# Layer opening of a two-layer mixer step: filter tiles waited for one by one in a new order, the adaLN bias on GpSimd, the first filter network in halves, no copy of x

## The chip, the cores and the metric

The kernel runs on one core of a Trainium2 chip. The metric is the device time of one execution in microseconds; of before there are three runs. The engines are TensorE (PE), VectorE (DVE), ScalarE (ACT), GpSimd (POOL) and SyncE (SP, which here issues nearly all DMAs).

## What is computed

Two layers (DEPTH = 2) of a diffusion backbone over 1024 sample tokens and 128 prompt tokens, 1024 channels, float32. Each layer is one mixer with four groups (latent attention, grouped-query attention, differential attention, a Hyena long convolution). What matters here is the beginning of a layer:

```python
def hyena_filters(n, lp):
    feats = concatenate([t, cos(f * w), -sin(f * w)])                  # n x 33
    h = sin(freq[0] * (feats @ fw1 + fb1))                             # n x 64
    h = sin(freq[1] * (h @ fw2 + fb2))                                 # n x 64
    h = (h @ fw3).reshape(n, 2, 2, 256)                                # two orders, forward and backward
    return h * exp(-t * abs(decay))

mod = silu(c) @ ada_w[i] + ada_b[i]                                    # shift, scale, gate; once for c, once for c_ctx
h = rmsnorm(x, norm_pre) * (1.0 + scale) + shift
out = mixer(h, ...)                                                    # its Hyena part convolves with the filters by FFT
x = x + gate * rmsnorm(out, norm_post)
```

The output is x after both layers, and some keys and values of the prompt.

## The kernel before

Tokens lie in nine tiles of 128: tile t < 8 holds the sample tokens with residue t modulo 8, tile 8 (NT) the prompt. One SBUF area, the arena, holds nearly everything at fixed offsets. PSUM has eight banks, which TensorE claims in turn (`K.claim`, `K.next`): a claim waits until the bank's last user has been drained. Each engine has its own program, in a fixed order; semaphores join them.

The opening of a layer has these steps.

*Network.* Two small products (`network_product`, K = 33 and 64), each followed on VectorE by scaling and a range reduction (`network_angle`: tensor_scalar, tensor_scalar, three scalar_tensor_tensor, tensor_scalar, each waited for) and on ScalarE by a sine (L1302). The 1152 tokens lie as 2 x 576 columns; the arithmetic runs over all 576 at once, though the products come in 512 and 64. For layer 1 the network runs inside the output stage of layer 0, beside the output products of tiles 4 and 6.

*Decays.* ScalarE makes exp(-t |decay|) of each tile: Abs (L1307), nine Exp (L1309). In layer 0 after the sines, in layer 1 after the last square of layer 0.

*Filter transforms.* For order o = 1 and then 0, TensorE multiplies the nine tiles with fw3, tiles 0 to 8 in sequence, jobs `("f3", o, t)`. VectorE (`filter_rows`) multiplies each bank with the decay (L1722) and, for even t, folds forward and backward part into difference and sum (two more L1722); tiles 0 and 8 have a small memset (L1828) in between. For odd t ScalarE negates the backward part (L1321).

*Filter spectra.* For each order 8 banks `("FE", o, a0, p)`, a0 = 0 to 3 and p = 0, 1, and a prompt bank `("FEp", o)`. a0 even reads tiles a0 and a0 + 4; a0 odd reads all four odd tiles, with the negated parts. TensorE starts them once all tiles are ready:

```python
pe.wait_ge(*S.at("filter_negated", o))
pe.wait_ge(*S.at("filter_folded", (o, NT)))
```

ScalarE drains the banks scaled (L1335, L1340). After order 1, VectorE and GpSimd add and subtract the quarters (`butterfly`) into a spectrum that is stored away; ScalarE drains order 0 only after that.

*Modulation.* ada(j), j = 0 to 5, multiplies silu(c) with 512 columns of ada_w; its left operand is csil, spread at L1764 and L1765 over 256 columns of the arena in each layer. ada(0) follows the transforms of order 1, ada(1) to (3) lie between its spectrum banks, ada(4) and (5) in order 0. VectorE adds the bias (`add_ada_bias`) over 128 partitions, of which GpSimd had cleared all (L2381) and SyncE filled two; SyncE waits for the clearing with ada_b and what is queued behind. Small products bring shift and scale onto partitions (job modT), and, before the last FE pair of order 0, the gates onto rows (`gate_row`), which VectorE multiplies with norm_post (`gate_rows`) and SyncE stores away (gates_kept).

*x.* Six of nine rows tiles are loaded (`load_x`), squared on ScalarE (L1315), scaled on VectorE (`normalize`, with a power on GpSimd), turned by TensorE (`x_turned`) and modulated by ScalarE (L1347) and VectorE (`modulate`, L1806) into hT. The first product of the Hyena input, `hyena_input(0, 0)`, needs tiles 0 to 3. In layer 0 x is first copied by DMA into the output xs[0], and read from there. SyncE loads x rows 6 to 8 after the store of the gate rows.

## Time and profile before

| what | us |
|---|---|
| median of three runs | 2441.25 (2438.95 to 2441.79) |
| profiled execution | 2435.95 |
| its span | 2434.2 |
| TensorE busy | 2272.0 (93%) |
| VectorE, ScalarE, GpSimd busy | 1317.5, 935.4, 253.8 |

Layer 0 opens with the span; its first product of the Hyena input starts at 123.09. Layer 1 opens at 1220.6. In a row of the timeline, the first number is the start from the beginning of the span, the second the time to the end of what is merged in the row; in brackets stands how long the engine was idle before it, and what ended that. L1722, L2336 and L659 are helpers (tensor_tensor of VectorE and of GpSimd, matmul): the tiles and shapes tell one use from another. A float32 matmul stands as two records of MATMUL.

### The profile page before, as it was taken

How to read it: one execution, taken by the hardware profiler on the slowest of the kernel's cores; microseconds unless marked ns; L12 is line 12 of the kernel's file. 1: busy time of each engine (PE TensorE's matmuls, PEld its weight loads, DVE VectorE, ACT ScalarE, POOL GpSimd, SP SyncE). 2: the span in 40 equal slices, each digit the busy share in tenths (PEclk: the TensorE clock that was granted, in tenths of full speed). 3: DMA queues.
4: the chain of work that ended last, by engine and by line, in shares of the span. 5: the costliest groups of instructions: out<-in, count | busy, mean ns of one | idle time of the engine just before them, and what ended most of it. 6: DMA issues, size and time to landing. Idle time of an engine off the chain costs nothing. (4 is left out here: it accounts for less than half of the span.)

```text
span 2434.2 us, 36385 instructions
## 1 busy us (share of the span) xinstructions
PE 2272.0 (93%) x14536; PEld 1599.2 (66%) x14536; DVE 1317.5 (54%) x2454; ACT 935.4 (38%) x1924; POOL 253.8 (10%) x400
## 2 busy tenths in 40 slices
PE   6999999899999998989999999998999999889898
PEld 3656865685477776864856577657854777768657
DVE  3642764564656466583446337545645654855732
ACT  2332113553155265483224221135521652744721
POOL 0310001000100011011304000010011000110213
PEclk9999999999999999999989999999999999999999
DMA  8710100100020000113275101001001100001022
GB/s 282 262 46 29 57 18 1 54 2 15 2 76 2 4 4 7 36 36 131 79 233 203 53 11 57 18 1 54 1 15 37 41 1 8 1 7 71 1 87 87
DMA packets 75150, 129.64 MB, mean 53 GB/s; under 512 B 25794, under 2 KB 38978, under 8 KB 73348
## 3 DMA queue, kind: packets, MB, share of 16 engines
q1 hardware_dynamic: 73960, 121.65, 14.6%
q10 hardware_dynamic: 1024, 5.67, 0.7%
q8 instruction: 117, 1.92, 0.3%
q14 instruction: 49, 0.40, 0.1%
HBM read 110.10 MB, written 21.92 MB: 54 GB/s over the span
## 5 line engine op out<-in xcount | busy, mean ns | idle before, releaser
L659 PE MATMUL psum<-arena 128*32 128x128 f32 (+9 forms) x9392 | 1505.3, 391 | 63.0 <-issue 11.9
L659 PEld LDWEIGHTS psum<-arena 128*32 128x32 f32 (+3 forms) x9392 | 930.5, 151 | 564.5 <-issue 423.7
L663 PE MATMUL psum<-ident,arena 128*128 128x128 f32 (+1 forms) x2248 | 335.2, 279 | 70.8 <-ACT arena L1543 34.0
L1722 DVE TENSOR_TENSOR arena<-arena 128x256 f32<-128x256 f32 (+10 forms) x710 | 318.8, 493 | 146.6 <-ACT arena L1419 42.6
L663 PEld LDWEIGHTS psum<-ident,arena 128*128 128x128 f32 (+1 forms) x2248 | 254.3, 141 | 155.6 <-issue 101.9
L659 PE MATMUL psum<-k_parts,q_parts 96*128 96x384 f32 (+2 forms) x1000 | 269.8, 366 | 17.1 <-ACT arena L1454 6.0
L2019 DVE TENSOR_REDUCE st<-psum 128x1 f32<-128x1152 f32 (+1 forms) x144 | 177.9, 1237 | 52.3 <-PE psum L659 52.1
L1722 DVE TENSOR_TENSOR arena<-psum,arena 128x512 f32<-128x512 f32 (+2 forms) x116 | 68.1, 596 | 253.3 <-PE psum L659 253.1
L2114 DVE TENSOR_REDUCE st<-psum 128x1 f32<-128x1152 f32 (+1 forms) x144 | 174.0, 1235 | 53.6 <-PE psum L659 53.1
L659 PEld LDWEIGHTS psum<-k_parts,q_parts 96*128 96x128 f32 (+1 forms) x1000 | 171.0, 193 | 34.7 <-issue 16.8
L1454 ACT ACTIVATE arena<-psum,st 128x1152 f32<-128x1152 f32 (+1 forms) x144 | 162.4, 1128 | 51.8 <-DVE st L2019 43.7
L1529 ACT ACTIVATE arena<-psum,st 128x1152 f32<-128x1152 f32 (+1 forms) x144 | 162.5, 1129 | 34.0 <-DVE st L2114 33.6
L1469 ACT COPY arena<-psum 128x512 f32<-128x512 f32 (+1 forms) x244 | 102.1, 433 | 184.9 <-PE psum L663 184.8
L2336 POOL TENSOR_TENSOR st<-st,minus 128x1 f32<-128x1 f32 x72 | 43.7, 607 | 798.2 <-ACT arena L1529 798.2
L2336 POOL TENSOR_TENSOR arena<-arena 128x1024 f32<-128x1024 f32 (+2 forms) x38 | 98.6, 2603 | 189.1 <-DVE arena L1855 138.7
L2033 DVE COPY arena<-psum 128x512 f32<-128x512 f32 (+1 forms) x156 | 93.6, 612 | 28.7 <-PE psum L663 28.7
L1543 ACT COPY arena<-psum 128x512 f32<-128x512 f32 (+1 forms) x200 | 90.3, 470 | 46.4 <-PE psum L663 45.4
L1886 DVE SCALAR_TENSOR_TENSOR arena<-arena,hcw 128x1024 f32<-128x1024 f32 x24 | 30.8, 1285 | 125.9 <-ACT arena L1373 125.5
L2124 DVE SCALAR_TENSOR_TENSOR arena<-arena,st 128x1152 f32<-128x1152 f32 (+1 forms) x72 | 93.0, 1291 | 9.8 <-POOL st L2336 9.8
L1492 ACT ACTIVATE arena<-psum 128x512 f32<-128x512 f32 x36 | 21.5, 598 | 173.3 <-PE psum L659 173.3
L2336 POOL TENSOR_TENSOR st<-st,mhalf 128x1 f32<-128x1 f32 (+2 forms) x72 | 56.2, 780 | 300.8 <-DVE st L1727 300.8
L1653 ACT CAST q_parts<-psum 96x512 fp32r<-96x512 f32 (+1 forms) x54 | 31.7, 588 | 117.0 <-PE psum L663 116.5
(146 smaller groups left out, 1685.8 us busy)
## 6 DMA issues: line engine op xcount, KB each, us to landing
arena<-in_ada_w SPq DMA_DIRECT2D x12, 2048.0 KB, 8.3
arena<-in_w_in SPq DMA_DIRECT2D x10, 2048.0 KB, 9.6
arena<-out_xs SPq DMA_DIRECT2D x36, 512.0 KB, 5.9
out_xs<-arena SPq DMA_DIRECT2D x18, 512.0 KB, 2.6
arena<-in_w_out SPq DMA_DIRECT2D x4, 2048.0 KB, 8.0
out_xs<-in_x ACTq DMA_DIRECT2D x1, 4608.0 KB, 19.2
spectrum_kept<-arena SPq DMA_DIRECT2D x2, 2304.0 KB, 8.6
arena<-spectrum_kept SPq DMA_DIRECT2D x2, 2304.0 KB, 8.4
```

What stands on the lines that cost most here:

```text
L659: return nc.tensor.matmul(out, lhsT, rhs, start=start, stop=stop)
L663: return nc.tensor.transpose(out, src, ident[0:n, 0:n])
L1454: nc.scalar.activation(at(buf, nk, w), psum[:, 512 * b0:512 * (b0 + nk)].rearrange("p (c n) -> p c n", c=nk)[:, :, 0:w], ACT.Exp, bias=st[ ...
L1469: nc.scalar.copy(at(SLOTS[grp] + slot(grp, u) * 1152 + 512 * j, nk * P), bank[b][:, 0:nk * P]).then_inc(*S.up("turned_scalar", (grp, number)))
L1529: nc.scalar.activation(at(buf, nk, w), psum[:, 512 * b0:512 * (b0 + nk)].rearrange("p (c n) -> p c n", c=nk)[:, :, 0:w], ACT.Exp, bias=st[ ...
L1543: nc.scalar.copy(at(SLOTS[grp] + slot(grp, u) * 1152 + 512 * j, nk * P), bank[b][:, 0:nk * P]).then_inc(*S.up("turned_scalar", (grp, number)))
L1722: return nc.vector.tensor_tensor(out, a, b, op)
L2019: nc.vector.tensor_reduce(st[:, 16 + x % 4:17 + x % 4], psum[:, 512 * b0:512 * (b0 + nk)].rearrange("p (c n) -> p c n", c=nk)[:, :, 0:w], ...
L2033: nc.vector.tensor_copy(at(SLOTS[grp] + slot(grp, u) * 1152 + 512 * j, nk * P), bank[b][:, 0:nk * P]).then_inc(*S.up("turned_vector", (grp ...
L2114: nc.vector.tensor_reduce(st[:, 16 + x % 4:17 + x % 4], psum[:, 512 * b0:512 * (b0 + nk)].rearrange("p (c n) -> p c n", c=nk)[:, :, 0:w], ...
L2124: nc.vector.scalar_tensor_tensor(p0, p1, c, p0, ALU.mult, ALU.add).then_inc(*S.up("mixed", (grp, u)))
L2336: return nc.gpsimd.tensor_tensor(out, a, b, op)
```

## The change

- The nine tiles are taken in the order 2, 6, 0, 4, 8, 1, 5, 3, 7 (FILTER_ORDER), the spectrum products in the order 2, 0, 1, 3 (FE_ORDER). An even a0 waits only for tile a0 + 4 folded, an odd one for tile 7 and the negations. The prompt's product stands after the second a0, which in order 1 ScalarE's negations of tiles 3 and 7 follow too.
- ScalarE drains ada(j), GpSimd adds the bias over two partitions. The clearing memset and its wait are gone; ada_b is loaded after the last output product of the layer before.
- The gate rows are made after all spectrum banks of order 0, and on VectorE after `normalize` of six tiles.
- The silu columns of layer 1 are made in the output stage of layer 0, at another place in the arena. A table load for Exp is asked for after the second sine there.
- The first network runs in two halves of 288 columns. The decay row and negt are loaded first on ScalarE's queue, and in layer 0 the decays are made ahead of the sines; tanh for silu follows the sines, and VectorE finishes silu at the prompt tile of order 1.
- x isn't copied: layer 0 reads the input itself, and xs has two instead of three entries. `load_x` waits for tile 7 of order 0 instead of tile 8.

```diff
+FILTER_ORDER = (2, 6, 0, 4, NT, 1, 5, 3, 7)
+FE_ORDER = (2, 0, 1, 3)
-HALF_PARTS = ((0, 512), (512, HALF - 512))
+HALF_PARTS = ((0, HALF // 2), (HALF // 2, HALF // 2))
...
 # SyncE
-                sp.wait_ge(*S.at("ada_bias_cleared"))
+                if l >= 1:
+                    sp.wait_ge(*K.full(("y", NT, 1), 1))
                 for s in range(2):
-                    load(at(A_ADAB, 3072, parts=1, base=s), lay("ada_b"), "ada_params")
+                    load(at(A_ADAB, 3072, parts=1, base=s), lay("ada_b"), "ada_bias")
...
-                if l == 0:
-                    sp.wait_ge(S.raw("x_copied"), 16)
-                else:
+                if l >= 1:
...
-                sp.wait_ge(*K.emptied(("f3", 0, NT)))
+                sp.wait_ge(*K.emptied(("f3", 0, FILTER_ORDER[-1])))
...
 # TensorE
-                    for t in range(TT):
+                    for t in FILTER_ORDER:
...
-                    pe.wait_ge(*S.at("filter_negated", o))
-                    pe.wait_ge(*S.at("filter_folded", (o, NT)))
-                    for a0 in range(4):
+                    for turn, a0 in enumerate(FE_ORDER):
                         back = (4 - a0) % 4
-                        if o and a0 % 2:
-                            ada((a0 + 1) // 2)
-                        if o == 0 and a0 == 2:
+                        if a0 % 2:
+                            pe.wait_ge(*K.emptied(("f3", o, 7)))
+                            pe.wait_ge(*S.at("filter_negated", o))
+                        else:
+                            pe.wait_ge(*S.at("filter_folded", (o, a0 + 4)))
+                        if o and turn % 2:
+                            ada((turn + 1) // 2)
+                        if o == 0 and turn == 2:
                             ada(5)
...
+                        if turn == 1:
+                            pe.wait_ge(*S.at("filter_folded", (o, NT)))
+                            ps = claim(("FEp", o), K.next())
...
+                    else:
+                        pe.wait_ge(*S.at("ada_biased", 5))
+                        for s in range(2):
+                            for half in range(2):
+                                ps = claim(("gate_row", s, half), K.next())
...
 # ScalarE
+            load_decay(act, 0, "decay_params")
+            act.dma_start(negt[:, :], I["negt"]).then_inc(*S.up("decay_params", None, 16))
             load_rest(act, 0, "first_rest")
+            act.wait_ge(*S.all("decay_params"))
+            decays()
+            for n in (1, 2):
+                for i, (c, w) in enumerate(HALF_PARTS):
+                    act.wait_ge(*S.at("first_angle", (n, i)))
+                    nc.scalar.activation(at(F_ARG + c, w), at(F_ARG + c, w), ACT.Sin).then_inc(*S.up("first_sine", (n, i)))
             act.wait_ge(S.raw("constants"), 16 * N_CONST)
             nc.scalar.activation(csil[:, :, :], craw[:, :, :], ACT.Tanh, scale=0.5).then_inc(S.raw("silu_ready"), 1)
-            act.dma_start(xs[0], I["x"]).then_inc(S.raw("x_copied"), 16)
...
+                def take_ada(j):
+
+                    act.wait_ge(*K.full(("ada", j)))
+                    nc.scalar.copy(mod[:, j * 512:(j + 1) * 512], B(("ada", j))).then_inc(*K.drained(("ada", j)))
...
+                    take_ada(0 if o else 4)
                     if o == 0:
+                        negate((1, 5, 3, 7))
...
+                        if o and turn == 0:
+                            negate((1, 5))
+                        if turn == 1:
+                            if o:
+                                negate((3, 7))
+                            act.wait_ge(*K.full(("FEp", o)))
+                            nc.scalar.mul(at(B2 + 4096, 512), B(("FEp", o)), 1.0 / N_PROMPT).then_inc(*K.drained(("FEp", o)))
+                    if o:
+                        take_ada(3)
...
+                            if n == 2:
+                                nc.scalar.preload_act_table_set("natural_log_exp_and_others")
...
 # VectorE
                 filter_rows(1)
-                add_ada_bias(0)
-                add_ada_bias(1)
-                add_ada_bias(2)
-                add_ada_bias(3)
                 filter_rows(0)
-                add_ada_bias(4)
                 for o in (1, 0):
                     if o == 0:
                         modulation()
-                        add_ada_bias(5)
-                        gate_rows()
                         for t in range(RING):
                             normalize(t)
+                        gate_rows()
...
 # GpSimd
-                nc.gpsimd.memset(at(A_ADAB, 3072), 0.0).then_inc(*S.up("ada_bias_cleared"))
+                def bias_ada(j):
+
+                    pool.wait_ge(*S.at("ada_bias"))
+                    pool.wait_ge(*K.emptied(("ada", j)))
+                    m = at(A_MOD + j * 512, 512, parts=2)
+                    tt(m, m, at(A_ADAB + j * 512, 512, parts=2), ALU.add).then_inc(*S.up("ada_biased", j))
+
                 for o in (1, 0):
+                    for j in range(4) if o else (4,):
+                        bias_ada(j)
```

## Rows read from the trace of the kernel before

**Rows 1.** The page: busy us, share of the span, instructions.
```profile
PE 2272.0 (93%) x14536; PEld 1599.2 (66%) x14536; DVE 1317.5 (54%) x2454; ACT 935.4 (38%) x1924; POOL 253.8 (10%) x400
```
**Rows 2.** Windows: busy PE, PEld, DVE, ACT, POOL; clock, DMA share, GB/s.
```profile
0.00:23.60 23.60, 4.37 (x16) 1.52 (x16) 10.14 (x19) 4.14 (x6) 2.99 (x7) 1.00 0.88 282
23.60:43.40 19.80, 19.74 (x37) 5.90 (x37) 11.11 (x22) 6.86 (x16) 0.00 (x0) 1.00 0.98 315
43.40:82.00 38.60, 38.60 (x190) 24.07 (x186) 11.52 (x22) 6.79 (x13) 0.00 (x0) 1.00 0.68 220
...
1220.60:1229.00 8.40, 7.48 (x19) 2.65 (x18) 6.81 (x7) 5.97 (x13) 5.50 (x3) 1.00 1.03 377
1229.00:1239.40 10.40, 5.64 (x19) 1.12 (x19) 9.84 (x21) 1.67 (x4) 0.00 (x0) 0.50 0.76 230
```
**Rows 3.** Timeline of layer 0's opening: start, us, engine, instruction, idle before.
```profile
7.40 2.19 PE L659 MATMUL psum<-arena 33*64 33x512 f32 x8 [7.40 <-DMA fwp<-in_hy_freq]
...
14.80 0.68 ACT L1302 ACTIVATE arena<-arena 128x576 f32<-128x576 f32 x1 [1.44 <-DVE arena L1738]
...
23.66 17.22 PE L659 MATMUL psum<-arena 64*128 64x512 f32 x24 [5.94 <-ACT arena L1302]
...
45.99 0.60 ACT L1335 ACTIVATE arena<-psum 128x512 f32<-128x512 f32 x1 [6.65 <-PE psum L659]
```
**Rows 4.** Groups by form, 0 to 45 us: busy us, mean ns, idle before.
```profile
L1737 DVE SCALAR_TENSOR_TENSOR arena<-arena 128x576 f32<-128x576 f32 x6 | 4.5, 758 | 0.2
...
L1309 ACT ACTIVATE arena<-arena,negt 128x256 f32<-128x256 f32 x9 | 3.7, 494 | 0.0
...
L1746 DVE TENSOR_SCALAR arena<-psum,fwp 128x512 f32<-128x512 f32 x2 | 1.6, 810 | 12.8 <-PE psum L659 12.8
...
L1296 ACT ACT_TABLE_LOAD x1 | 1.3, 1283 | 6.2 <-issue 6.2
...
L1735 DVE TENSOR_SCALAR arena<-arena 128x576 f32<-128x576 f32 x2 | 0.9, 460 | 0.1
...
L1307 ACT ACTIVATE arena<-arena 128x256 f32<-128x256 f32 x1 | 0.4, 398 | 0.0
```
**Rows 5.** Timeline of layer 1's opening, 1220 to 1245 us.
```profile
1220.61 7.47 PE L659 MATMUL psum<-arena 64*128 64x512 f32 x18
...
1223.99 2.35 POOL L2336 TENSOR_TENSOR arena<-arena 128x1024 f32<-128x1024 f32 x1 [1.58 <-DVE arena L2084]
1224.16 4.81 DVE L1765 COPY arena<-csil 128x16 f32<-128x16 f32 x1
...
1226.29 2.66 POOL L2381 MEMSET arena<- 128x3072 f32 x1
...
1229.41 0.88 DVE L1722 TENSOR_TENSOR arena<-arena 128x256 f32<-128x256 f32 x2
...
1231.05 3.64 PE L659 MATMUL psum<-arena 128*32 128x512 f32 x16
...
1238.26 0.88 DVE L1722 TENSOR_TENSOR arena<-arena 128x256 f32<-128x256 f32 x2
...
1239.40 12.97 PE L659 MATMUL psum<-arena 128*128 128x256 f32 x58 [4.71 <-DVE arena L1722]
...
1244.74 0.60 ACT L1335 ACTIVATE arena<-psum 128x512 f32<-128x512 f32 x1 [1.05 <-PE psum L659]
```
**Rows 6.** Timeline of layer 0: a negation, modT, the end of the opening.
```profile
75.48 0.42 ACT L1321 ACTIVATE arena<-arena 128x256 f32<-128x256 f32 x1 [4.93 <-DVE arena L1722]
...
97.69 0.16 DVE L1780 COPY mcol<-psum 128x16 f32<-128x16 f32 x1
...
117.65 5.51 DVE L1806 TENSOR_SCALAR arena<-psum,mcol 128x128 f32<-128x128 f32 x17
...
123.09 8.80 PE L659 MATMUL psum<-arena 128*128 128x512 f32 x16 [3.36 <-DVE arena L1806]
```
**Rows 7.** The page's DMA issues: KB each, us from issue to landing.
```profile
gates_kept<-arena SPq DMA_DIRECT2D x2, 1024.0 KB, 14.0
```

More of the change, by code:

```diff
@@ L156 @@
 SPLIT_W = {"gqa": 896, "diff0": 768, "diff1": 768}
-N_CONST = 6
+N_CONST = 5
 BARRIERS = 5
@@ L695, in ada @@
                     weights("ada", j)
-                    if j == 0:
+                    if j == 0 and l == 0:
                         pe.wait_ge(*S.at("silu_columns"))
+                    elif j == 0:
+                        pe.wait_ge(*S.at("silu_columns", "next", 1))
                     ps = claim(("ada", j), K.next())
@@ L721, in _ @@
                     else:
-                        for j in range(4):
-                            pe.wait_ge(*K.emptied(("ada", j)))
+                        if l == 0:
+                            pe.wait_ge(S.raw("constants"), 16 * N_CONST)
+                        pe.wait_ge(*S.at("ada_biased", 3))
                         ps = claim(("modT",), K.next())
@@ L1330, in _ @@
                             act.wait_ge(*S.all(f"x_stored{i}", 1))
-                    for a0 in range(4):
+                    for turn, a0 in enumerate(FE_ORDER):
+                        if o and turn % 2:
+                            take_ada((turn + 1) // 2)
+                        if o == 0 and turn == 2:
+                            take_ada(5)
                         for p in range(2):
@@ L1749, in _ @@
[L1749 to L1765 removed]
+                    network_angle(n, "first_step", "first_angle", (n, i), c, w)
@@ new lines, in silu_columns, with silu @@
+            def silu_columns(key):
+                link(nc.vector.memset(at(A_CSIL, KD * 32), 0.0))
+                nc.vector.tensor_copy(at(A_CSIL, KD, 32)[:, :, 0:2], csil[:, :, :]).then_inc(*S.up("silu_columns", key))
+            def silu():
+                v.wait_ge(S.raw("silu_ready"), 1)
+                nc.vector.scalar_tensor_tensor(csil[:, :, :], csil[:, :, :], 1.0, craw[:, :, :], ALU.add, ALU.mult
+                                               ).then_inc(S.raw("silu_ready"), 1)
+                v.wait_ge(S.raw("silu_ready"), 2)
+                nc.vector.tensor_scalar(csil[:, :, :], csil[:, :, :], 0.5, None, ALU.mult).then_inc(S.raw("silu_ready"), 1)
+                v.wait_ge(S.raw("silu_ready"), 3)
+                silu_columns(None)
@@ L2324, in _ @@
                                 v.wait_ge(*K.emptied(job))
-                            network_angle(n, "vector_step", "angle")
+                            network_angle(n, "vector_step", "angle", n)
+                    if t == NETWORK_AT[1] and l + 1 < DEPTH:
+                        silu_columns("next")
         @block.gpsimd
```

112 lines of the change are left out of this document (47 added, 65 removed).

## The prediction

> **What bounds the kernel now.** Read the page's busy rows first: TensorE is busy 93% of the span [rows 1], so only TensorE's idle or slowed stretches can give time back. The view by windows then compares them [rows 2]. The first 23.6 us hold 4.37 us of TensorE work. In the opening of layer 1, TensorE works 5.64 us of the 10.4 us to 1239.40, and the granted clock is at 0.50 (the 1.2 GHz level) in all of them. In the stretch from 23.60 TensorE is never short of work, but its records are long: the same 18 records of the transforms that take 7.47 us in layer 1 [rows 5] make up most of the 24 that take 17.22 us from 23.66 [rows 3]. So it runs at the lower level too, although the clock column says 1.00 there.
>
> The timelines say who ends the idle stretches. At the start: products, VectorE's angle arithmetic, a sine, the second products, again VectorE and a sine, and only then the filter transforms [rows 3]. In layer 1 the transforms end at about 1228.9 and the last filter tile is folded at 1239.14 (1238.26 + 0.88), 0.26 us before TensorE resumes [rows 5]. VectorE folds one even and one odd tile per 2.1 us (8.85 us for four pairs and one memset), but it has finished its first tile only when GpSimd's memset ends at 1228.95: its tiny copy of csil, begun at 1224.16, lasts 4.81 us beneath GpSimd's add and memset. The 4.71 us wait at 1239.40 is for tiles that the first spectrum product doesn't read.
>
> **Part 1: the filter spectrum in layer 1.** The memset, the copy and VectorE's clearing leave this place (the latter two run at tile 4 of the output stage, beside TensorE's output products; without that cover they would cost up to the 4.81 us of the copy). The tile order is 2, 6, 0, 4, prompt, 1, 5, 3, 7. VectorE is free at about 1223.9 (the copy's start, less its 0.3 us of clearing) and starts tile 2. A product takes 0.6 us (a pair's 2.1 us hold two of them and 0.88 us of folds); the folds read two SBUF tensors and wait for GpSimd's add of x, 1223.99 to 1226.34 [rows 5]. They end at 1227.2, tile 6 at 1228.7, tile 0 at 1230.5 (it has the memset), tile 4 at 1232.0, the prompt tile at 1233.8 and the four odd tiles, 0.6 each, at 1236.2.
>
> TensorE: by 7.47/18 a record of 512 columns takes 0.42 us and one of 256 half of it; a matmul has two, so an even spectrum bank (four matmuls of 256) takes 1.7 us and the prompt's, two, 0.86 with its start. Eight tiles to 1228.08, the ninth 0.83 more (2 x 7.47/18), say 1228.9; ada(0) takes half of 3.64 us if the clock holds, 1230.8. Tile 6 was folded at 1228.7, so product (1, 2) starts at 1230.8. The next ask tile 4 after 3.4 us, at 1234.2 (ready 1232.0), then the prompt's, then tile 7: all ready. The start moves from 1239.40 to 1230.8: 8.6 us. Before, the first two banks ended at 1244.74 (when ScalarE takes the second) where 3.44 us at the full clock would give 1242.9: 1.8 us for the low clock, also saved if the clock doesn't fall.
>
> Against this stands a new wait. In spectrum 1 the negation of tiles 3 and 7 sits on ScalarE behind the drain of the fourth bank: 0.1 + 0.5 + 0.42 + 0.42 = 1.45 us [rows 5, 6], while TensorE has only the prompt product, 0.86 us, before it asks for them. Queued behind that wait are product 1 and everything after it: 0.6 us per layer. Bounds 0 and 1.0; I take 0.6. Layer 1 gives 8.6 + 1.8 - 0.6 = 9.8 us. Bounds: if the clock falls in the transforms anyway (it fell at 1229.0 after an idle of 0.97 us, which now goes; the second transforms of layer 0, between 43.4 and 82 us, ran through at 1.00 [rows 2]), ada(0) costs 1.8 us more and the 1.8 isn't saved, 6.2 us; if contention costs VectorE nothing, nothing is added, since TensorE is the bound.
>
> The Trainium skill, SBUF — State Buffer, "SBUF: two separate sides", calls the port pair that VectorE and GpSimd share an exclusive lock: an instruction of VectorE with two SBUF inputs and a GpSimd one that reads SBUF shut each other out for their whole length. The trace agrees in the copy that waits out both GpSimd instructions [rows 5]. It speaks against biases on GpSimd: each 2 x 512 add could stop VectorE's folds. By that rule the add for ada(0), an estimated 1.3 us by the 2.35 us for 1024 columns halved, moves tile 4 to 1233.3, still ahead of 1234.2: the sum stays. By bounds without it: 0 to 1.3 us of VectorE, 0 of TensorE.
>
> **Part 2: the network in halves, layer 0.** Per half of 288 columns: the read from PSUM 0.58 us (0.81 at 512, less 224 columns at 1.04 ns), three tensor_scalar at 0.31 (0.46 at 576, less 288 columns at half of STT's 1.04 ns), three scalar_tensor_tensor at 0.46 (0.76 less 288 x 1.04 ns), 0.15 between them: 2.95 us [rows 4]. Product half 0 ends at about 8.6 (half of 2.19 after 7.40) and VectorE does 8.6 to 14.5 for n = 1. ScalarE is the catch: it issued nine loads before its first table load at 6.2 [rows 4] and now ten, to 6.8; then come that load (1.28), Abs (0.40) and nine Exp (3.7), to 12.3, and the sine's table, 13.6. The first half sine ends at 14.05, its product at 15.2, VectorE works to 21.1, the last sine ends at 21.65 and the transforms start at 21.7 instead of 23.66: 2.0 us. If Abs and Exp need two tables it is 0.7; if ScalarE weren't late, 2.7. I take 2.0: in the trace Abs ran with no load ahead of it [rows 4]. Loads still land in time: only the first parameters at 7.40 hold TensorE, and two more small transfers ahead on ScalarE's queue could move that by 0 to 0.3 us. I take 0.
>
> All this is ahead of work at the low clock. The clock rose not in the transforms but some 1.7 us after the spectrum products began at 43.4: their first bank came at 45.99, 2.6 us instead of 1.72 [rows 3], so 1.7 us of it ran at half speed; if it rises with the products again, the 2.0 us come through whole; if up to 1.7 us later, 0.8 less. The new wait costs 0.6 here too. Layer 0: 2.0 - 0.6 = 1.4 us, 0 to 2.5.
>
> **Part 3: edits that I cost at nothing.** ada(j) drained by ScalarE (0.6 us each, idle there) and biased by GpSimd: modT asks for it some 10 us after ada(3). VectorE loses its adds of some 0.6 us, none of them waited for. The modT bank is asked for again by the second bank of product 1, about 99.9 by the old clock; VectorE reads modT at 97.7 [rows 6], less the bias add gone ahead of it: 2 us to spare. The four gate rows (3.4 us of TensorE) move behind the spectrum products, and on VectorE behind six normalisations. ScalarE's last square comes 2.6 us earlier, but VectorE then has four products of 0.6 us to do before the bias and modulate(0), which began at 117.65 and sets TensorE's start at 123.09 [rows 6]. 2.6 against 2.5: 0 (-0.6 to 1.0 per layer). The copy of x held nobody: TensorE never waited for a load after 7.40. Its going is worth 0; between 0 and the 0.6 us of its issue.
>
> **Sum.** 9.8 + 1.4 = 11.2 us. The profiled execution took 2435.95 (span 2434.2); it becomes 2424.8. The three runs of before have their median 5.3 us above it, so the forecast is 2441.25 - 11.2 = 2430.0.
>
> **Rivals.** (A) The clock falls in layer 1 all the same, and rises late in layer 0: 6.2 + 0.6 = 6.8 us, 2434.5. For it: it fell once in just these 8.4 us of 64-row matmuls. Against: there was an idle moment right before, and layer 0 shows none. (B) The order doesn't do what it says: some other wait (a bank, a lock) makes TensorE wait for all nine tiles. Then the start is at 1236.2 and at the low clock: 3.2 - 0.6 + 1.4 = 4.0 us, 2437.2. Against it: the banks asked for are drained before the times above. (C) The gate rows make it slower. SyncE stands behind their drain, at about 116.5 now, with the store of them and behind it x rows 6 to 8. If the store holds the loads back for its whole time to land, 14.0 us [rows 7], and row 6, of half its size, takes half as long, row 6 is there at 137.5; a square and the scaling make some 3 us, so x_turned(6) starts at 140.5 where TensorE wants it at 131.9, the end of the product begun at 123.09 [rows 6]: 8.6 us per layer, 17.2 in both, less the gain 6.0 us slower: 2447. It decides from row 6 landing 12.4 us after the store's issue, and eats the gain from 18. Against it: one queue's transfers overlap, and ahead of the store stand weights that will have landed by then.
> (D) More than I count: the gate rows give 1.0 per layer, 0.6 of stall is 0: 2426.8.
>
> **How the numbers follow.** Forecast 2430.0: 0.55. A 0.20, B 0.08, C 0.04, D 0.13. The range: A and D inside, plus 1 us for the spread of the runs (2438.95 to 2441.79): 2425.0 to 2436.5. Outside lie B, C and the tails. This measurement can tell about 0.2%, 4.9 us, from no change. The forecast, D and nearly all of A clear that; B stands just below it and C is beyond. Faster 0.87, same 0.10, slower 0.03.
>
> **What would show it.** Right: the transforms start near 21.7, ScalarE's nine Exp come before its sines; in layer 1 no memset on GpSimd, product (1, 2) 8 to 9 us earlier after the last stage's end, clock at 1.00 throughout; a stall of 0.6 us in front of product 1 ended by ScalarE's negation; modulate(0) as long after the transforms as before. Wrong: a clock of 0.50 after ada(0), TensorE waiting for a fold or the first half sine ended by a second table load, or a wait for x row 6.

## The result and the profile after

The kernel after takes 2409.38 us (median of 4 runs, 2406.51 to 2414.31) where the kernel before takes 2440.1 in the same comparison (2436.34 to 2441.79): ratio 0.9877, 95% interval 0.9858 to 0.9895, some 30 us faster. Forecast were 2430.0 and a range down to 2425.0; the direction was right, the size was not.

The profiled execution after is the slowest of its four (2414.31; span 2412.5), that of before (2435.95; span 2434.2) is below all four of its own, so the two traces show 21.7 us. The repeat below, profiled in one of its fastest runs (span 2404.9), is read beside them. The page's busy rows: TensorE is busy 15.8 us less with the same 14536 instructions [rows 1].

```profile
PE 2256.2 (94%) x14536; PEld 1595.1 (66%) x14536; DVE 1307.9 (54%) x2454; ACT 942.1 (39%) x1939; POOL 264.2 (11%) x410
```

Equal instructions with less busy time mean that single records became shorter or lay over each other. The timeline of TensorE in the two openings of the kernel after (start, us, engine, instruction, idle time before it and who ended it):

```profile
5.89 2.19 PE L666 MATMUL psum<-arena 33*64 33x288 f32 x8 [5.89 <-DMA fwp<-in_hy_freq]
14.19 2.18 PE L666 MATMUL psum<-arena 64*64 64x288 f32 x8 [6.11 <-ACT arena L1322]
22.14 22.36 PE L666 MATMUL psum<-arena 64*128 64x512 f32 x88 [5.77 <-ACT arena L1322]
44.98 25.50 PE L666 MATMUL psum<-arena 128*128 128x256 f32 x132 [0.48 <-issue]
...
1215.12 5.76 PE L666 MATMUL psum<-arena 64*128 64x512 f32 x20
1222.34 11.94 PE L666 MATMUL psum<-arena 128*32 128x512 f32 x68 [1.46 <-DVE arena L1767]
1234.76 25.50 PE L666 MATMUL psum<-arena 128*128 128x256 f32 x132 [0.48 <-issue]
...
1301.28 1.69 PE L666 MATMUL psum<-arena 128*128 128x512 f32 x2 [2.44 <-DVE arena L1852]
```

To be seen: the transforms of layer 1 are 20 records in 5.76 us. Before, 18 took 7.47, and two more followed behind a wait [rows 5]. The wait of 4.71 us for the last folds is gone; in its place stand 1.46 us for a bank that VectorE drains late and, in front of the first odd product, 0.48 us. The weight loads of the same stretch mark where each piece starts:

```profile
1215.11 0.30 PEld L666 LDWEIGHTS psum<-arena 64*128 64x128 f32 x4 [0.35 <-issue]
1215.65 0.19 PEld L666 LDWEIGHTS psum<-arena 64*128 64x128 f32 x1 [0.23 <-issue]
...
1218.03 0.30 PEld L666 LDWEIGHTS psum<-arena 64*128 64x128 f32 x4 [0.81 <-issue]
1218.57 0.19 PEld L666 LDWEIGHTS psum<-arena 64*128 64x128 f32 x2 [0.24 <-issue]
...
1222.30 0.19 PEld L666 LDWEIGHTS psum<-arena 128*32 128x32 f32 x8 [2.26 <-issue]
...
1224.19 3.32 PEld L666 LDWEIGHTS psum<-arena 128*128 128x128 f32 x16 [0.84 <-issue]
```

Four loads lie in 0.30 us, where before two did and the others followed one by one, 0.43 us apart:

```profile
1220.61 0.29 PEld L659 LDWEIGHTS psum<-arena 64*128 64x128 f32 x2 [0.35 <-issue]
1221.14 0.19 PEld L659 LDWEIGHTS psum<-arena 64*128 64x128 f32 x1 [0.24 <-issue]
```

The first spectrum product (the last row of the kernel after) starts 9.08 us after the first transform; before it was 18.79 (1239.40 less 1220.61). No window of this stretch is at the low clock any more:

```profile
1215.10:1224.20 9.10, 7.64 (x38) 2.44 (x37) 7.28 (x13) 4.69 (x12) 2.90 (x2) 1.00 1.03 381
1224.20:1234.40 10.20, 10.08 (x56) 7.08 (x52) 6.34 (x13) 4.63 (x10) 2.56 (x2) 1.00 1.06 371
```

From such rows comes this account. The opening of layer 0 runs from 0, that of layer 1 from its first transform, both to the first Hyena product:

```
us                                   before    after    repeat
layer 0: first transform              23.66    22.14    22.14
  nine transforms                     16.14    10.41    10.09
  ada(0)                               3.57     1.86     1.86
  second nine transforms               8.26     5.69     5.69
  first Hyena product at              123.09   113.14   110.88
layer 1: transform to first product   18.79     9.08     9.07
  second nine transforms               8.26     5.69     5.69
  length of the opening                99.50    86.16    86.16
both openings                          222.6    199.3    197.0
rest of the span                      2211.6   2213.2   2207.9
```

The openings give 23.3 us (25.6 in the repeat). The rest holds little of the change (layer 1's silu columns, a table load and the reading of x in layer 0's output stage), and its length goes with the clock: outside the openings the clock is low for 51 us in the trace of before, 56 in that of after and 48 in the repeat (summed over windows of 2 us).

### The profile page after: what moved, and what is told of

It is laid out like the page before. It is cut to its first block and busy times, and to the rows that moved or that the text cites. A ratio compares the mean times of both kernels' runs of the same rounds, so it can differ in the third digit from the quotient of the medians.

```text
span 2412.5 us, 36410 instructions
## 1 busy us (share of the span) xinstructions
PE 2256.2 (94%) x14536; PEld 1595.1 (66%) x14536; DVE 1307.9 (54%) x2454; ACT 942.1 (39%) x1939; POOL 264.2 (11%) x410
## 5 line engine op out<-in xcount | busy, mean ns | idle before, releaser
L666 PE MATMUL psum<-arena 128*32 128x128 f32 (+9 forms) x9392 | 1486.3, 389 | 57.3 <-issue 12.9
L1767 DVE TENSOR_TENSOR arena<-psum,arena 128x512 f32<-128x512 f32 (+2 forms) x104 | 57.2, 564 | 235.4 <-PE psum L666 235.4
L2380 POOL TENSOR_TENSOR arena<-arena 128x1024 f32<-128x1024 f32 (+3 forms) x50 | 114.4, 2294 | 169.1 <-ACT arena L1332 83.0
L2166 DVE SCALAR_TENSOR_TENSOR arena<-arena,st 128x1152 f32<-128x1152 f32 (+1 forms) x72 | 92.9, 1291 | 10.1 <-POOL st L2380 10.1
```

What stands on the lines that cost most here:

```text
L666: return nc.tensor.matmul(out, lhsT, rhs, start=start, stop=stop)
L1767: return nc.vector.tensor_tensor(out, a, b, op)
L2166: nc.vector.scalar_tensor_tensor(p0, p1, c, p0, ALU.mult, ALU.add).then_inc(*S.up("mixed", (grp, u)))
L2380: return nc.gpsimd.tensor_tensor(out, a, b, op)
```

## The experiments

"Before" in each comparison is the kernel before on the same chip; its medians lay between 2438.6 and 2439.8.

**The kernel after again.** The same file, to have a second trace and a time on the chip of the next three.

> The changed kernel once more, to see how much of its gain is in every execution: its traced execution shows the two openings shorter by 10.0 us (first Hyena input product at 113.14 instead of 123.09) and 13.3 us (1215.12 to 1301.28 instead of 1220.61 to 1320.11), 23.3 in all, while the medians lie 30 us apart. If the rest is chance of where the clock falls between the openings: again about 0.988 of before, and a trace whose openings take 113 and 86 us within 1 us. If something outside the openings is faster: a stage between them is shorter in this trace too.

2408.13 us (2406.69 to 2410.33), ratio 0.9871 [0.9851, 0.9891]. The gain holds, and so do the openings to within 0.1 us, but for 2.3 us in layer 0. There the trace after has 6.8 us at the low clock from 73 us on, where the repeat has none.

**Tiles in another order.**

```diff
-FILTER_ORDER = (2, 6, 0, 4, NT, 1, 5, 3, 7)
+FILTER_ORDER = (2, 0, 4, 6, NT, 1, 3, 5, 7)
```

> The changed kernel with the tile order 2, 0, 4, 6, prompt, 1, 3, 5, 7: the same waits, and each spectrum product can start as early as before, but tiles whose transform uses the upper 64 rows of TensorE (0 to 3) no longer alternate with those on the lower 64 (5 to 8). Theory R (the gain I didn't count is overlap of transforms on different row halves): the 9 transforms of an order take again about 8 us at the full clock instead of 5.5, and about 16 instead of 10.4 in layer 0, where the clock then rises late again: 12 to 17 us slower than the changed kernel, near 2424. Theory W (all comes from waiting for single tiles and from the missing memset): within 2 us of the changed kernel.

2421.08 us (2417.03 to 2423.54), ratio 0.9918 [0.9903, 0.9934]: 13 us slower than the order of the change. The time by itself doesn't tell the theories apart: tile 6, which the first product asks for, is now fourth, and in layer 1 TensorE waits 2.37 us for it, which the text above had not allowed for.

```profile
1215.40 6.61 PE L666 MATMUL psum<-arena 64*128 64x512 f32 x20
...
1226.91 11.72 PE L666 MATMUL psum<-arena 128*128 128x256 f32 x52 [2.37 <-DVE arena L1767]
```

The length of the transforms does. In the second block of either layer nine tiles take 8.26 us with the old order, 6.54 with this one and 5.69 with that of the change: 0.86 us less for each tile that runs beside one of the other half, two tiles here and three there. Which tiles these are can be read from the trace, since each sets the semaphore of its bank. In the kernel after they are 2 and 6, prompt and 1, 5 and 3. Here they are 6 and 1, prompt and 3: tile 1 is done 0.85 us before the prompt tile, which stands ahead of it in the program. The overlap reaches past a neighbour of the same half. Tile 4, which uses both halves, ran beside no other tile.

**The new order alone, in the kernel before.**

```diff
                 for o in (1, 0):
-                    for t in range(TT):
+                    for t in FILTER_ORDER:
```

(and the same in VectorE's folds and ScalarE's decays; TensorE still waits for all nine tiles)

> The kernel before with only the tile order 2, 6, 0, 4, prompt, 1, 5, 3, 7 for transforms, filter rows and decays; the spectrum products still wait for all tiles. Theory R: layer 0 gains 5.7 us in its first transforms, 2 to 3 us in the second, and up to 4 us from the earlier rise of the clock; layer 1 gains 1 to 3 us (VectorE ends the wait there): 10 to 14 us faster than before. Theory W: within 2 us of before.

2428.95 us (2427.52 to 2431.56), ratio 0.9955 [0.994, 0.9969]. One edit that my sum had at nothing gives 10 us. TensorE in layer 0, and at the first product of layer 1:

```profile
23.64 9.87 PE L660 MATMUL psum<-arena 64*128 64x512 f32 x20 [5.94 <-ACT arena L1303]
36.98 13.27 PE L660 MATMUL psum<-arena 128*32 128x512 f32 x62 [3.46 <-DMA arena<-in_ada_w]
...
1238.01 38.23 PE L660 MATMUL psum<-arena 128*128 128x256 f32 x184 [5.02 <-ACT arena L1322]
```

The transforms of layer 0 end some 6 us earlier, and now TensorE waits 3.46 us for ada's weights: no load had held it there before. Layer 1's opening is no shorter (99.94 us against 99.50): the odd tiles now come last, and TensorE, which still awaits all, stands 5.02 us for ScalarE's negations of them. So only 2.4 of the 9.9 us lie in the openings of this trace (220.2 against 222.6); the others are in the rest of the span, where this kernel's work is that of before, and are not explained.

**All nine tiles awaited, in the kernel after.**

```diff
+                    pe.wait_ge(*S.at("filter_folded", (o, NT)))
+                    pe.wait_ge(*K.emptied(("f3", o, 7)))
                     for turn, a0 in enumerate(FE_ORDER):
```

> The changed kernel, but the spectrum products of each order wait again for all tiles drained and folded. What the single waits are worth: by the trace of the changed kernel the last tile of order 1 is done at 1230.9 in layer 1, where the products start at 1224.2, and at 36.0 in layer 0, where they start at 34.4: 6.6 + 1.6 = 8 us slower than the changed kernel if the clock holds, 3 us more if the new idle of 6 us makes it fall. Were the waits worthless (the row halves alone make the gain): within 1 us.

2428.87 us (2424.69 to 2433.27), ratio 0.9953 [0.9936, 0.9969]. TensorE in layer 1:

```profile
1214.68 5.75 PE L666 MATMUL psum<-arena 64*128 64x512 f32 x20
1221.90 1.92 PE L666 MATMUL psum<-arena 128*32 128x512 f32 x16 [1.47 <-DVE arena L1769]
1230.59 9.65 PE L666 MATMUL psum<-arena 128*128 128x256 f32 x37 [6.77 <-issue]
```

The first product starts 15.9 us after the first transform (1230.59 less 1214.68) instead of 9.08. The opening is 96.87 us long instead of 86.16. Of the 3.9 us beyond those 6.8, 2.8 come from a stretch at the low clock that follows the wait, most of the others from a wait of 0.93 us further on. In layer 0 the first product waits 1.95 us, and the first Hyena product comes at 115.48 instead of 110.88. So waiting for each product's own tiles is worth 20.7 us with the new order (2428.87 less 2408.13), 15.4 of them in the openings of the traces (212.4 against 197.0).

**The same, with the tiles in sequence.**

```diff
-FILTER_ORDER = (2, 6, 0, 4, NT, 1, 5, 3, 7)
+FILTER_ORDER = tuple(range(TT))
```

> The kernel after, with the first spectrum product waiting for all nine tiles (as in the run that took 2428.87) and the transforms in the order 0, 1, ..., 7, prompt, so that neighbours use the same rows of the array. It differs from that run by the order alone. Theory (transforms overlap when neighbours use different halves of the array's rows): a block of nine takes about 8.3 us again instead of 5.7 at the full clock, and some 16 instead of 10.4 us in layer 0's first block, where ada(0) also falls back to the low clock (3.6 us instead of 1.86). Layer 0 first block +5.7 +1.7 less the 1.9 us that TensorE waited there for folds, the second block of each layer +2.6 each, layer 1's first block about 0 (there VectorE's folds are the bound): +10.7, about 2439.5 us. Rival (the order matters only for which tile is ready first, which the added wait has already switched off): the blocks keep 5.7 and 10.4 us and the time stays at 2429.

2439.76 us (2429.8 to 2445.16, 12 runs), ratio 1.0 [0.9988, 1.0013]. It differs from the last kernel by the order of the tiles alone, and from the forecast of the overlap theory by 0.3 us, which is partly luck: its runs spread over 15 us. The order is worth 10.9 us between the medians and 8.0 in the openings of the traces (220.4 against 212.4). Its weight loads in layer 1, one tile after the other:

```profile
1226.16 0.29 PEld L666 LDWEIGHTS psum<-arena 64*128 64x128 f32 x2 [0.35 <-issue]
1226.70 0.19 PEld L666 LDWEIGHTS psum<-arena 64*128 64x128 f32 x1 [0.24 <-issue]
...
1234.42 0.16 PEld L666 LDWEIGHTS psum<-arena 128*32 128x32 f32 x8 [0.76 <-issue]
```

Nine transforms take 8.26 us at the full clock (1226.16 to 1234.42) and 16.2 us in layer 0's first block (22.13 to 38.32). This kernel still has every other edit of the change: the halves, the biases on GpSimd, the gate rows at the end, no memset and no copy of x. Together they are worth nothing measurable without the order and its waits (the interval is some 3 us to either side).

**The copy of x back, in the kernel after.**

```diff
             decays()
+            act.dma_start(outs["x_copy"], I["x"]).then_inc(S.raw("x_copied"), 16)
...
+                if l == 0:
+                    sp.wait_ge(S.raw("x_copied"), 16)
```

> The kernel after, with a 4.6 MB copy of x (into a tensor that nobody reads) issued by ScalarE after its decays, and SyncE waiting for it before it loads x, as before. Theory (the copy now competes with ada's first weights, because the transforms are shorter): TensorE waits for ada's weights before ada(0) in layer 0, which starts at 34.5 to 37 instead of 32.3 us; 2 to 4.5 us, 2410.5 to 2412.5. My prediction's view (the copy holds nobody): ada(0) stays at 32.3 and the time at 2408 to 2409.

2413.78 us (2411.66 to 2415.26), ratio 0.9897 [0.9882, 0.9911]: 5.65 us more than the kernel after, above the range expected.

```profile
22.14 9.45 PE L668 MATMUL psum<-arena 64*128 64x512 f32 x20 [5.77 <-ACT arena L1325]
36.11 13.83 PE L668 MATMUL psum<-arena 128*32 128x512 f32 x68 [4.51 <-DMA arena<-in_ada_w]
```

The wait is 4.51 us, and the clock, which had risen in the transforms, is low again for 6.8 us from 33 on; the first Hyena product comes at 116.65 instead of 110.88.

**No copy of x, in the kernel before, in the old and in the new order.**

```diff
-            act.dma_start(xs[0], I["x"]).then_inc(S.raw("x_copied"), 16)
...
+                def x_rows(t):
+                    if l == 0:
+                        return I["x"][rows(t), :]
```

> The kernel before, with layer 0 reading x itself: no 4.6 MB copy of x, nothing else changed. Theory (the copy costs only where the transforms are short enough for ada's weights to be late; in the kernel before TensorE reached ada(0) at 39.80, behind the weights' landing at about 37): no change, 2438 to 2440. Rival (the copy's traffic costs something in any order): 2434 or less.

2436.87 us (2430.66 to 2444.08, 12 runs), ratio 0.999 [0.9977, 1.0003]: no change that can be told. TensorE reaches ada(0) at 40.8, long after its weights. But the edit did a second thing:

```profile
14.52 1.28 ACT L1303 ACT_TABLE_LOAD   x1 [2.98 <-DVE arena L1739]
```

ScalarE's table load for the sine, which began at 12.08 behind the copy's issue, now begins at 14.52, behind the wait for the angle. The sine comes 1.0 us later and the transforms start at 24.67 instead of 23.66. What the going of the copy alone gives back is set against that.

> The kernel before, with the new tile order and no copy of x; all nine tiles are still awaited. Theory (overlap and copy hang together): the wait of 3.46 us for ada's weights goes, ada(0) starts at about 33.7 and the clock rises there instead of falling back, as the copy cost 5.65 us in the kernel after; the first Hyena product of layer 0 comes near 114.5 instead of 120.2, and the time is about 2423. Rival (the two edits add up: alternating 9.9, copy 0): 2429.

2428.25 us (2424.62 to 2429.0), ratio 0.9946 [0.9932, 0.9961], where 2423 was expected. The wait for the weights is gone, ada(0) starts at 34.17 at the full clock, but the transforms start at 25.04 instead of 23.64, by the same table load, and another wait has taken the place of the first:

```profile
36.29 0.42 ACT L1323 ACTIVATE arena<-arena 128x256 f32<-128x256 f32 x1 [5.99 <-DVE arena L1724]
37.48 1.03 ACT L1323 ACTIVATE arena<-arena 128x256 f32<-128x256 f32 x3 [0.78 <-DVE arena L1724]
38.61 1.64 PE L662 MATMUL psum<-arena 128*128 128x256 f32 x4 [2.51 <-ACT arena L1323]
```

ScalarE's negations of the odd tiles, which all products still await, end at 38.5 and hold TensorE 2.51 us. The first Hyena product comes at 117.95, 2.3 us earlier than with the copy (120.21), though the medians lie only 0.7 us apart. So in the kernel before, in either order, the copy's cost is too small to be told, with the later table load against it; it is 5.65 us once order and waits are both there: a load that hides behind one wait shows when the last of them is gone.

**The memset back, in the kernel after.**

```diff
+                nc.gpsimd.memset(at(A_ADAB, 3072), 0.0).then_inc(*S.up("ada_bias_cleared"))
...
+                sp.wait_ge(*S.at("ada_bias_cleared"))
```

> The kernel after, with GpSimd's memset of ada's bias rows back at the opening and SyncE's load of them behind it. Theory (VectorE's folds stand beneath GpSimd's add and memset): in layer 1 the folds end 2.3 us later each, TensorE waits some 2 us before its first spectrum product (1224.2 becomes about 1226.2) and the time is about 2410. Rival (ada(0) and the drains cover it): the first product does not move, 2408. In layer 0 nothing changes by either.

2408.63 us (2405.6 to 2410.4), ratio 0.9876 [0.9861, 0.9891]: no cost. The rival held. Layer 1 of this kernel:

```profile
1216.40 2.36 POOL L2381 TENSOR_TENSOR arena<-arena 128x1024 f32<-128x1024 f32 x1 [1.58 <-DVE arena L2127]
1216.90 2.60 DVE L1768 TENSOR_TENSOR arena<-arena 128x256 f32<-128x256 f32 x2
1218.69 2.67 POOL L2426 MEMSET arena<- 128x3072 f32 x1
...
1220.13 0.89 DVE L1768 TENSOR_TENSOR arena<-arena 128x256 f32<-128x256 f32 x2
```

Two folds beneath GpSimd's add take 2.60 us, two beneath the memset 0.89, as with nothing beside them. The folds have two SBUF inputs, and so are the case of the exclusive lock that the prediction quotes. The small copy of before, which it took as the sign of that lock, has one, and it also waited out the memset, which reads nothing [rows 5].

**The network in one piece.**

```diff
-HALF_PARTS = ((0, HALF // 2), (HALF // 2, HALF // 2))
+HALF_PARTS = ((0, 512), (512, HALF - 512))
```

(and one angle and one sine for each step)

> The kernel after, with the first network of layer 0 in one piece again (banks of 512 and 64 columns, one angle and one sine per step). My prediction's term: the halves give 2.0 us, so the transforms start about 2 us later, near 24.1. Rival: TensorE's first product now starts 1.5 us earlier for another reason (the first parameters land at 5.89 instead of 7.40), and that, not the halves, gave most of the 1.5 us seen; ScalarE's decays keep the first sine at 13.6 in either form, so the transforms start at about 22.5, 0.4 us later than the 22.14 of the kernel after.

One run, 2414.06 us. What counts is where the transforms start:

```profile
14.45 2.18 PE L666 MATMUL psum<-arena 64*64 64x512 f32 x8 [6.36 <-ACT arena L1321]
22.57 7.68 PE L666 MATMUL psum<-arena 64*128 64x512 f32 x14 [5.93 <-ACT arena L1321]
```

22.57 against 22.14: the halves give 0.43 us, not 2.0. The rival held to 0.1 us.

**What lets the first parameters land 1.5 us earlier.** First negt's load moved behind three others on SyncE, then, in another kernel, ScalarE's load of the decays, and negt's taken over from SyncE, put ahead of ScalarE's others as in the kernel after; both from the kernel before.

```diff
-            sp.dma_start(negt[:, :], I["negt"]).then_inc(S.raw("constants"), 16)
             sp.dma_start(sel[:, :, :], I["sel"]).then_inc(S.raw("constants"), 16)
             sp.dma_start(ident[:, :], I["ident"]).then_inc(S.raw("constants"), 16)
             sp.dma_start(halves[:, :], I["halves"]).then_inc(S.raw("constants"), 16)
+            sp.dma_start(negt[:, :], I["negt"]).then_inc(S.raw("constants"), 16)
```

> The kernel before, with SyncE's load of negt (128 rows of 36 bytes) moved behind those of sel, ident and halves. Theory (that load, of many small pieces and 2.25 us of issue, is what held the landing of the first parameters): TensorE's first product starts at 5.9 instead of 7.40 and the transforms at 22.2 instead of 23.66. Rival (the landing depends on what ScalarE's queue carries ahead, which this leaves as it was): 7.4 and 23.66.

> The kernel before, with ScalarE issuing the loads of the decays and of negt ahead of its others, as in the kernel after (in layer 1 the decays' load goes first as well, on SyncE). Theory (ScalarE's first loads, the small column loads into fwp and the 256 KB of weights, compete with SyncE's for the same DMA engines, and the first parameters land later for it): with them 0.9 us later TensorE's first product starts at 5.9 instead of 7.40. Rival: another difference sets the landing (GpSimd's memset at the start, or the load of ada's biases): 7.4.

One run each, 2439.11 and 2439.12 us. The first still starts at 7.44, so negt's place on SyncE is not it. The second starts at 5.89:

```profile
5.89 2.18 PE L660 MATMUL psum<-arena 33*64 33x512 f32 x8 [5.89 <-DMA fwp<-in_hy_freq]
15.42 2.19 PE L660 MATMUL psum<-arena 64*64 64x512 f32 x8 [7.35 <-ACT arena L1303]
23.55 7.19 PE L660 MATMUL psum<-arena 64*128 64x512 f32 x8 [5.94 <-ACT arena L1303]
```

And ScalarE's tanh in the same kernel:

```profile
12.68 0.22 ACT L1297 ACTIVATE csil<-craw 128x16 f32<-128x16 f32 x1 [4.53 <-DMA halves<-in_halves]
```

SyncE issues its six loads at the same times in both; ScalarE's order decides when they land. Alone it gives nothing: the angle is ready at 13.2, but the sine starts at 14.68, and the transforms at 23.55 as before. The tanh shows why. It stands ahead of the sines there and behind them after the change, and waits for the constants until 12.68; the copy's issue and the sine's table load follow. Moving the tanh alone was not tried.

**The gate rows back in their old place.**

```diff
+                        if o == 0 and turn == 3:
+                            pe.wait_ge(*S.at("ada_biased", 5))
+                            ... (the four gate rows)
```

(and VectorE takes them ahead of its normalisations)

> The kernel after, with the four gate rows back between the last two residues of the spectrum on TensorE, and ahead of the normalisations on VectorE (GpSimd adds ada(5)'s bias ahead of its six roots). My prediction priced the move of the gate rows at 0 (-0.6 to 1.0 us per layer): 2407 to 2410. Rival (the move gave part of the 10 us that the prediction missed): 2 us or more per layer, 2412 and above, with the first Hyena product as much later after the second transforms. The transforms' own shortening is untouched by this.

2423.81 us (2422.98 to 2427.27), ratio 0.9938 [0.9926, 0.9951]: 15.7 us more than the kernel after. My 0 is right against the kernel before and wrong for the kernel after. Layer 0 of this kernel:

```profile
88.03 1.58 ACT L1371 ACTIVATE arena<-psum 128x512 f32<-128x512 f32 x3 [13.19 <-DVE arena L1910]
...
92.51 0.61 ACT L1332 COPY arena<-psum 128x512 f32<-128x512 f32 x1
...
93.26 1.26 POOL L2380 TENSOR_TENSOR arena<-arena 2x512 f32<-2x512 f32 x1 [2.95 <-ACT arena L1332]
...
96.08 0.69 DVE L1767 TENSOR_TENSOR arena<-psum,arena 128x512 f32<-128x512 f32 x1 [8.07 <-PE psum L666]
```

```profile
88.07 3.72 PE L666 MATMUL psum<-arena 128*128 128x256 f32 x16 [1.13 <-DVE mcol L1827]
94.78 5.37 PE L666 MATMUL psum<-arena,sel 128*128 128x512 f32 x8 [2.99 <-POOL arena L2380]
```

ada(5) is done on TensorE at 83.2, but ScalarE, which now drains it, stands until 88.03 behind VectorE's butterflies, and gets to it at 92.51 behind five drains and two squares; GpSimd's bias follows, and the gate rows wait 2.99 us for it. They then run partly at the low clock, VectorE stands 8.07 us behind them, and the normalisations come late: the first Hyena product moves by 5.7 us in layer 0 (116.60 against 110.88) and as much in layer 1, 11.4 of the 15.7 us. By this chain ScalarE's drain is at no cost only because the gate rows moved behind it; the old drain with the old place of the gate rows was not tried in this kernel.

**Sines ahead of the decays; and the negation moved too.**

```diff
-            act.wait_ge(*S.all("decay_params"))
-            decays()
             for n in (1, 2):
             ... (the four half sines)
+            act.wait_ge(*S.all("decay_params"))
+            decays()
```

```diff
+                            if o and turn == 1 and p == 0:
+                                negate((3, 7))
...
-                            if o:
-                                negate((3, 7))
                             act.wait_ge(*K.full(("FEp", o)))
```

> The kernel after, with ScalarE's nine decays behind its four half sines of layer 0 instead of ahead of them. Theory (ScalarE's decays held the first half sine 3.3 us, from 10.34 when its angle was ready to 13.60): the first half sine starts near 10.4, VectorE is then never idle in the network, the transforms start near 19.3 instead of 22.14, and TensorE may meet ada's weights, which land near 29.5, for at most 0.5 us. All of it is ahead of work at the low clock; 2.3 to 2.9 us, 2405 to 2406. Rival (the decays then come too late for VectorE's first filter tile, or the clock rises later by what the start moved): transforms at 19.3, but the first spectrum product of layer 0 stays at 34.1 and the time at 2408.

> The kernel of the sines-first run, and ScalarE negates tiles 3 and 7 between its two drains of turn 1 in spectrum 1 instead of behind the prompt's. Theory: the wait of 0.48 us in front of the first odd product (44.98 in layer 0, 1234.76 in layer 1) goes in both layers: 1.0 us less than the sines-first run. Rival (the negations delay the drain of the second bank, whose bank TensorE asks for soon after): a wait of the same size in another place, the same time as the sines-first run.

2411.33 us (2408.84 to 2414.11), ratio 0.9884 [0.9868, 0.99], and 2411.8 us (2408.2 to 2413.53), ratio 0.9881 [0.9863, 0.9899]. Neither beats the kernel after. With the sines first the transforms start at 20.39 where 19.3 was expected, for the next wait is for a load:

```profile
12.42 1.23 PE L666 MATMUL psum<-arena 64*64 64x288 f32 x4 [4.34 <-DMA arena<-in_hy_bias]
13.87 1.22 PE L666 MATMUL psum<-arena 64*64 64x288 f32 x4 [0.23 <-ACT arena L1320]
20.39 9.21 PE L666 MATMUL psum<-arena 64*128 64x512 f32 x20 [5.29 <-ACT arena L1320]
```

The transforms start 1.75 us earlier, the first Hyena product comes at 109.05 instead of 110.88. In the second kernel TensorE runs from 20.82 on with no 0.48 us wait: that wait was ScalarE's negation, though the profile names no releaser. But the rest of the span is longer, and its mean clock lower. The repeat of the kernel after, then the sines-first kernel:

```profile
core 0: 2404.9 us, clock 0.989
```

```profile
core 0: 2411.6 us, clock 0.984
```

A gain of 1 to 2 us in one stage is below what the clock's scatter in the others leaves visible.

## Why the prediction was wrong

**The step that failed.** "By 7.47/18 a record of 512 columns takes 0.42 us" and "eight tiles to 1228.08, the ninth 0.83 more": I carried the duration of nine transforms over from the old order to the new one. That an order of tiles alters their duration stood in no term and no rival: the overlap of the transforms was priced at 0. The code says why it can: tiles 0 to 3 multiply in rows 0 to 63 of the array, 5 to 7 and the prompt's in rows 64 to 127, tile 4 in both; the new order alternates between the halves. All four blocks shrink: the second of either layer from 8.26 to 5.69 us, layer 1's first from 7.47 for eight tiles to 5.76 for nine, layer 0's first, mostly at the low clock, from 16.14 to 10.4 or 10.1. The two kernels that differ by the order alone show 10.9 us of the time (2439.76 to 2428.87), 8.0 of them in the openings. Most of the miss is in layer 0, whose opening gave 12.2 us in the repeat against 1.4 forecast; layer 1's gave 13.3 against 9.8. In the Trainium skill, TensorE: Matmul & The Clock Gate, "Part 3: Packing small matmuls — row/col tiling", small matmuls in different row groups of the array run at the same time, and a weight load passes a running matmul only where the row group differs. The traces agree (four loads in 0.30 us where two lay); I had read these rows for the clock and not for this.

**The clock in layer 0.** "If it rises with the products again": it rose in the transforms instead. ada(0) is at full speed after them, 1.86 us against 3.57, in every kernel with the alternating order whose TensorE did not wait for ada's weights; in the kernel with tiles in sequence ada(0) starts at 38.32 and the first product at 41.92, 3.6 us, as before. So the alternation gives 5.7 and 1.7 us there, against my 0. And with transforms so short the single waits are worth something in layer 0 too, 4.6 us (115.48 to 110.88), where I had counted them in layer 1 alone.

**Layer 1, part 1.** But for the transforms' length the mechanism was right, place by place. The first product moves by 9.7 us by the time since the first transform (18.79 to 9.08), forecast 8.6; the difference is the shorter block, less the 1.46 us wait of ada(0) for a bank that VectorE drains behind tile 2. That wait I hadn't seen: my TensorE was slow enough not to meet it. The clock stays at 1.00, so the 1.8 us came too. The first fold is held beneath GpSimd's add as forecast. The negation's wait, forecast 0.6, is 0.48 in both layers.

**Layer 0, part 2.** 2.0 us forecast, 1.52 found, for other reasons. With the network in one piece the transforms start at 22.57, 1.09 earlier than before: that is the earlier landing of the first parameters (5.89 instead of 7.40, a term I had at 0 to 0.3 us the other way) together with ScalarE's new order, for the landing alone gave 0.1. The halves add 0.43. That ScalarE's decays hold the first half sine was right (13.60; its angle was ready at 10.34). A half's arithmetic takes 3.0 us, as its terms add up to; the 2.95 written was a slip.

**Part 3.** All costs forecast at 0 are 0 against the kernel before: the kernel with every edit but the tile order and its waits takes the same time as before. Two of them are 0 only in that company. "TensorE never waited for a load after 7.40" was true of a TensorE that came to ada(0) at 39.80; at 32.3 the copy costs 5.65 us. And the gate rows' move is what makes ScalarE's drain of ada(5) free, 15.7 us. "2 us to spare" for the modT bank is gone too: TensorE waits 1.12 us for it in the repeat. The memset, by contrast, would cost nothing now.

**The rivals.** A (the clock falls in layer 1 all the same) did not come. B (all tiles awaited) did not come, and built by hand it takes 2428.87 us, not 2437.2, since the overlap gives its 10.9 us there as well. C did not come: SyncE issues x row 6 0.38 us behind the store, ScalarE's square waits for it 0.56 us (1.89 in the repeat, 1.33 before), and TensorE doesn't. D had the right direction for other reasons: the stall is 0.48 us and not 0, and the gate rows' move gave nothing against the kernel before.

**What stays open.** The openings account for 25.6 of the 30.7 us between the medians of before and repeat. The other 5 lie in the rest of the span, which holds little of the change. There the clock is low for 51 us in the trace of before and 48 in the repeat, and one kernel's own runs differ as much: the kernel before without the copy ran from 2430.66 at a mean clock of 0.989 to 2444.08 at 0.982. Whether a shorter opening makes the clock fall less often later, the small edits there give something, or these medians differ by chance, the runs don't tell. Nor is it settled by what way ScalarE's order of loads delays SyncE's; only that it does.

## What to carry to other kernels

When a change reorders matmuls that use half of the array's rows, work out which half each uses before you carry their duration over; here a tile of one half that ran beside a tile of the other cost nothing more. An edit priced at 0 because something else hides it has that price only as long as the cover stands: write down when the cover ends, and see whether another edit of the same change ends it. To settle such shares, take all edits but one, as well as one alone: here the order alone gave 10 us by the medians, the waits on top of it 20, and the rest nothing without both.

## What was not expected of the hardware

- Order alone: nine 64-row transforms in fp32 take 5.69 to 5.76 us alternating and 8.26 in sequence; a transform of the other half ran 0.85 us ahead of one that stood before it in the program.
- GpSimd's memset of 128 x 3072 doesn't hold VectorE's adds of two SBUF tensors (two take 0.89 us beneath it), while GpSimd's add does (2.60). The small copy of before was held to the end of both [rows 5].
- The order in which ScalarE issues its loads moved the landing of SyncE's from 7.40 to 5.89 us, with SyncE's own issues unmoved.
- The same program's runs differ by 13 us with the mean granted clock (0.989 to 0.982).
